# Two gather rings of four slots, a denser selection and coefficients in two halves in a PEER decoder kernel

## What is computed

```
q  = (h @ wq), split by head and in two halves
s1, s2 = scores of the halves against 128 keys each
v1, i1 = top_k(s1, 16);  v2, i2 = top_k(s2, 16)
sc, ci = top_k(v1[:, None] + v2[None, :], 16)      # of 256 candidates
eidx = i1[ci // 16] * 128 + i2[ci % 16]
gate = softmax(sc)
z    = gelu(sum_d h[d] * u_tab[eidx, d])
out  = sum_k gate[k] * z[k] * v_tab[eidx[k], :]
```

## Time and profile before

| | us |
|---|---|
| three runs, median | 2764.75 |
| lowest, highest | 2763.35, 2766.94 |
| the profiled execution | 2765.24 |
| its span | 2763.5 |
| busy: PE, DVE, POOL, ACT | 1892.6, 1378.6, 1262.6, 994.6 |

### The profile page before, as it was taken

The page is one execution under the profiler, slowest core; times in us unless marked ns, Lnnn a source line. Parts: engine busy times, 40 slices in busy tenths (PEclk is TensorE's granted clock), DMA queues, the critical chain, the costliest instruction groups (busy, mean ns, idle before and its releaser), DMA issues.

```text
span 2763.5 us, 31979 instructions
## 1 busy us (share of the span) xinstructions
PE 1892.6 (68%) x10179; PEld 1554.4 (56%) x10179; DVE 1378.6 (50%) x3350; ACT 994.6 (36%) x1254; POOL 1262.6 (46%) x1216
## 2 busy tenths in 40 slices
PE   6998855555555555699589897799556554555556
PEld 3676744444444444576389896567445443445445
DVE  1033665656555555223752534726556565656552
ACT  2102344444444443513211111213444443444445
POOL 2000677777777767300000000005777676777774
PEclk8999956666565656799689897899666665656567
DMA  9743899999999999734100002327999998999996
GB/s 360 285 153 123 307 354 352 362 335 377 342 344 340 357 354 369 290 120 166 40 1 1 1 1 73 103 80 241 362 342 373 355 367 316 364 344 377 340 357 252
DMA packets 242654, 717.42 MB, mean 260 GB/s; under 512 B 39672, under 2 KB 45056, under 8 KB 242556
## 3 DMA queue, kind: packets, MB, share of 16 engines
q0 software_dynamic: 165888, 604.05, 58.8%
q1 hardware_dynamic: 62212, 105.00, 10.8%
q10 hardware_dynamic: 14456, 7.06, 1.0%
HBM read 712.38 MB, written 3.65 MB: 259 GB/s over the span
## 4 chain that ended last, share of the span: by engine, by line
PE 37%; DMA 23%; issue 15%; POOL 12%; DVE 7%; ACT 4%; POOLq 1%; SPq 0%; DVEq 0%; ACTq 0%
PE ps L557 14%; DMA ARENA<-in_peer_u,CURU 14%; POOL ARENA L1856 12%; DMA ARENA<-in_peer_v,CURV 8%; PE ps L646 7%; PE ps L774 5%; ACT ARENA L1105 3%; DMA W<-in_w_ada 1%; PE ps L756 1%; PE ps L534 1%; PE ps L520 1%; PE ps L510 1%; DMA W<-in_conv_w_in 1%; PE ps L619 1%; DVE ARENA L1594 1%
## 5 line engine op out<-in xcount | busy, mean ns | idle before, releaser
L646 PE MATMUL ps<-ident,ARENA 128*128 128x128 f32 x4608 | 932.2, 378 | 720.2 <-ACT ARENA L1105 719.6
L646 PEld LDWEIGHTS ps<-ident,ARENA 128*128 128x128 f32 x4608 | 793.3, 199 | 859.1 <-ACT ARENA L1105 828.6
L1856 POOL DMA_INDIRECT ARENA<-in_peer_u,CURU x576 | 595.3, 1034 | 1274.4 <-DVE ARENA L1415 1079.7
L1440 DVE SCALAR_TENSOR_TENSOR ARENA<-ARENA 128x1024 f32<-128x1024 f32 x576 | 703.9, 1225 | 665.0 <-DMA ARENA<-in_peer_u,CURU 643.7
L1105 ACT ACTIVATE ARENA<-ARENA,CF 128x1024 f32<-128x1024 f32 x576 | 647.7, 1144 | 789.1 <-DMA ARENA<-in_peer_v,CURV 562.5
L1856 POOL DMA_INDIRECT ARENA<-in_peer_v,CURV x576 | 651.3, 1131 | 191.1 <-issue 164.6
L557 PE MATMUL ps<-H,W 128*128 128x288 f32 x1024 | 256.2, 414 | 4.5 <-DVEq L1785 2.8
L557 PEld LDWEIGHTS ps<-H,W 128*128 128x128 f32 x1024 | 198.6, 195 | 60.2 <-DVEq L1785 3.0
L967 ACT ACTIVATE W<-ps 128x512 f32<-128x512 f32 (+2 forms) x97 | 55.8, 578 | 233.9 <-PE ps L774 173.6
L774 PE MATMUL ps<-W 128*128 128x128 f32 (+1 forms) x1088 | 129.7, 284 | 0.1
L774 PEld LDWEIGHTS ps<-W 128*128 128x128 f32 (+1 forms) x1088 | 127.5, 199 | 2.3 <-issue 0.9
(11 more groups left out here) (281 smaller groups left out, 1616.1 us busy)
## 6 DMA issues: line engine op xcount, KB each, us to landing
W<-in_w_ada SPq DMA_DIRECT2D x24, 2048.0 KB, 15.6
W<-in_peer_wq SPq DMA_DIRECT2D x8, 2048.0 KB, 8.3
W<-in_conv_w_in SPq DMA_DIRECT2D x6, 2048.0 KB, 18.2
ARENA<-in_peer_u,CURU POOLq DMA_INDIRECT x576, 6.1
ARENA<-in_peer_v,CURV POOLq DMA_INDIRECT x576, 6.1
W<-in_conv_w_out SPq DMA_DIRECT2D x2, 2048.0 KB, 7.9
W<-in_rwkv_wr SPq DMA_DIRECT2D x2, 2048.0 KB, 25.2
W<-in_rwkv_wk SPq DMA_DIRECT2D x2, 2048.0 KB, 10.2
```

Source lines behind the costliest of these rows:

```text
L646: m = pe.matmul(ps[:, acc + c // 4, c % 4 * P:(c % 4 + 1) * P], RVV[:, k % RING, c * P:(c + 1) * P], ident[:], start=(first and k == 0 and ...
L1440: v.scalar_tensor_tensor(RU[:, k % RING, :], RU[:, k % RING, :], 1.0, h, ALU.mult, ALU.mult, accum_out=ZB[:, e, k:k + 1]).then_inc(s_z, 1)
L1856: pool.indirect_dma_start(ring[:, k % RING, :], None, tab, bass.IndirectOffsetOnAxis(ap=idx[:, k:k + 1], axis=0)).then_inc(landed[k % RING ...
```

## The change

`RING` becomes 4 for both rings. `SPAN` = 8 keeps the memory of before, so that no other buffer moves. The waits for landed tiles count four rounds of the ring in a unit. The choice gets two parts behind each of tiles 1 to 7 and behind tile 15, in place of one behind each of tiles 2 to 15. Gelu and coefficients come in halves of eight tiles: `gelu(u + 1, half 0)` ahead of V tile 10 of unit u, `coef(u + 1, half 0)` behind dot 14, the second halves at the start of the next unit (`coef` ahead of dot 3). ACT's exp comes ahead of V tile 13 in place of 14. ACT waits for the coefficients ahead of tiles 0 and 8.

```diff
-RING = 8
+RING = 4
+SPAN = 8
...
+                def gelu(u, e, half):
+                    h = slice(8 * half, 8 * half + 8)
+                    act.wait_ge(s_z, u * 16 + (8 * half + 8))
+                    act.activation(GL[:, e, h], ZB[:, e, h], ACT.Gelu).then_inc(s_gelu, 1)
+
+                gelu(u0, 0, 0)
+
                 def unit(u, lu, e, last):
-                    if not last:
+                    if last == 0:
 
                         act.wait_ge(s_sel, u * NSEL + NSEL)
                         act.sem_inc(s_actgo, 1)
                         act.activation(SCUR[:, e].rearrange("p a k -> p (a k)"), at(SCALL, lu + 2), ACT.Copy).then_inc(s_scur, 1)
-                    act.wait_ge(s_z, u * 16 + 16)
-                    act.activation(GL[:, e, :], ZB[:, e, :], ACT.Gelu).then_inc(s_gelu, 1)
-                    act.wait_ge(s_coef, u + 1)
+                    gelu(u, e, 1)
                     for k in range(TOPK):
-                        if k == 14 and not last:
+                        if k == 10 and last < 2:
+                            gelu(u + 1, 1 - e, 0)
+                        if k == 13 and last == 0:
                             gate_exp(u + 2, e)
-                        act.wait_ge(v_land[k % RING], u * 32 + 16 * (k // RING + 1))
+                        if k % 8 == 0:
+                            act.wait_ge(s_coef, u * 2 + (k // 8 + 1))
+                        act.wait_ge(v_land[k % RING], u * (16 * TOPK // RING) + 16 * (k // RING + 1))
...
                         for k in range(TOPK):
-                            if k == 2:
-                                coef(u, e)
+                            if k == 3:
+                                coef(u, e, 1)
                             if k == 8:
 
                                 v.wait_ge(s_sel, u * NSEL + 2 * NSEL)
                                 v.wait_ge(v_free, u * 16 + RING)
                                 v_indices(1 - e)
                             z_of(u + 1, k, 1 - e, at(HTOK, (lu + 1) // 8))
-                            if k >= 2:
+                            if k == 14:
+                                coef(u + 1, 1 - e, 0)
+                            if 1 <= k < 8 or k == 15:
+                                next(chosen, None)
                                 next(chosen, None)
                     else:
-                        coef(u, e)
+                        coef(u, e, 1)
                     for _ in chosen:
                         pass
-                def coef(u, e):
+
+                def coef(u, e, half):
+                    h = slice(8 * half, 8 * half + 8)
                     v.wait_ge(s_sel, u * NSEL + NSEL)
-                    v.wait_ge(s_gelu, u + 1)
-                    v.tensor_tensor(CF[:, e, :], GL[:, e, :], GATE[:, e], ALU.mult).then_inc(s_coef, 1)
+                    v.wait_ge(s_gelu, u * 2 + (half + 1))
+                    v.tensor_tensor(CF[:, e, h], GL[:, e, h], GATE[:, e, h], ALU.mult).then_inc(s_coef, 1)
+
+                coef(u0, 0, 0)
```

More of the change, by code:

```diff
@@ L144, in build @@
         W = sb("W", [WRING, DC, 512])
-        N_RV, N_ROWS, N_SEL = 2 * RING * D, 3 * D, 2880
+        N_RV, N_ROWS, N_SEL = 2 * SPAN * D, 3 * D, 2880
         ARENA = sb("ARENA", [N_RV + 2 * N_ROWS + N_SEL])
@@ L160, in build @@
         COUT = sb("COUT", [DC, 18])
-        rings = RV.rearrange("p (r s d) -> p r s d", r=2, s=RING)
+        rings = RV.rearrange("p (r s d) -> p r s d", r=2, s=SPAN)
         RU, RVV = rings[:, 0], rings[:, 1]
@@ L185, in build @@
         CROW = carve(N_RV + N_ROWS, [D])
-        KR = [carve(off, [2, HEADS, P]) for off in (RING * D + 2560, RING * D + 512)]
-        Q = carve(RING * D, [16, TOK])
-        KT = carve(RING * D + 16 * TOK, [2, HEADS, NKEYS])
+        KR = [carve(off, [2, HEADS, P]) for off in (SPAN * D + 2560, SPAN * D + 512)]
+        Q = carve(SPAN * D, [16, TOK])
+        KT = carve(SPAN * D + 16 * TOK, [2, HEADS, NKEYS])
         QP = carve(N_RV + N_ROWS, [16, P])
@@ L1108, in experts @@
                     for e in range(2):
-                        unit(i * 2 + (u0 + e), i * 2 + e, e, False)
+                        unit(i * 2 + (u0 + e), i * 2 + e, e, 0)
                 for e in range(2):
-                    unit(u0 + UNITS - 2 + e, UNITS - 2 + e, e, True)
+                    unit(u0 + UNITS - 2 + e, UNITS - 2 + e, e, 1 + e)
             def rwkv():
@@ L1437, in z_of @@
                 def z_of(u, k, e, h):
-                    v.wait_ge(u_land[k % RING], u * 32 + 16 * (k // RING + 1))
+                    v.wait_ge(u_land[k % RING], u * (16 * TOPK // RING) + 16 * (k // RING + 1))
                     v.scalar_tensor_tensor(RU[:, k % RING, :], RU[:, k % RING, :], 1.0, h, ALU.mult, ALU.mult,
```

## The result

The changed kernel takes 3145.4 us (median of 4 runs, 3141.7 to 3150.3) against 2764.1 us (2756.6 to 2766.9) for the kernel before: 1.140 times, 95% interval 1.137 to 1.143, or 381 us more. The forecast was 200 us more. The sign and the place are right; 180 us are missing, and the time lies 100 us outside the range.

The account below looks back on a forecast made before the run. The expert stages' gathers, copy engines 95% busy, were taken to bound the kernel. 31 x 1.41 + 9.6 gave 53.3 us a unit; with starts and tails 200 us more, 2765.24 + 200 = 2965 us, range 2895 to 3045.

Parts of the forecast that it names:

- The stand: Behind tile 7, DVE waits for ACT's exp and POOL stands at U12: 9.6 us between landings, 8.2 lost a unit.
- At 1.41 us a gather: Copy time of each 512 KB gather in the units, bounds 1.35 to 1.475; 31 of them plus 9.6 make 53.3 us.
- the first mark: First V index mark of layer 0: 363.9 against 338.97, 24.9 us late.
- the unit without a choice: Unit 16: dot 8 and U12 5.8 us, 22 gathers 31.0, dot 7 1.4; mark 16 at 1201.6.
- the prediction's own sum: Whole run: layer 0 93 us longer, 200 us together with layer 1, so 2965 us; chance 0.70.
- The tail: End of a layer, last dot to final reduction: V tiles alone turn in four slots, 4 us more than 24.7.
- Four slots bind nowhere in mid-unit: V slot held 9.6 us of an 11.3 us round, U slot 8.9: no cost counted in mid-unit.
- The rival of 3090 us: The four slots bind as well, V slots late in mid-unit: 125 us on top of 2965; chance 0.10.
- The halves: Gelu and coefficients in halves: ACT's 6.8 us wait goes, worth nothing by itself, but keeps four slots turning.
- The hole at the U indices: POOL's 3.3 us wait a unit goes with the denser selection: 45.1 us a unit, 2.1 to 3.1 us less.
- the rival "faster": Choice's last part falls on tile 15, so the exp wait costs nothing: 78 us gained, 2712 us; chance 0.05.
- The rival "copies run faster with fewer in flight": With four slots, copies run at 1.35 us a gather, worth 60 us: 2905 us; chance 0.10.

Follow-up runs that it names:

- the fastest kernel: Changed kernel with eight slots, the choice's last part behind tile 15 instead of 7, and h's rows copied to PSUM: 2562.8 us, 0.930 of the kernel before.

## Why the prediction was right in kind and 180 us short

**The stand: right.** The call behind tile 7 waits for the exp, DVE stands there in every unit with a choice, POOL stands at U12 (11.4 us, where I had about 9), and V12 to U12 is one chain without a copy under way. The last part behind tile 15 takes 369 us away. The term that was too small in the chain is POOL's wake-up: dot 8 is over at 489.48 and U12 is issued at 490.29, 0.8 us where I had 0.1 (from the exp to the gate sum it is 0.3 for 0.1); 10.5 us against 9.6, some 28 us over 32 units. The rows that would have told it stood in the trace of before, after the wait for L1415: DVE's L1415 ended at 739.85, POOL's gather began at 740.74.

```profile
739.68 0.17 DVE L1415 TENSOR_TENSOR ARENA<-ARENA 128x16 f32<-128x16 f32 x1
...
740.74 0.93 POOL L1856 DMA_INDIRECT ARENA<-in_peer_u,CURU  x1 [2.76 <-DVE ARENA L1415]
```

**"At 1.41 us a gather": this is the term that failed.** The period was worked out as 31 x 1.41 + 9.6, with 1.41 as what the copies can do. Measured, the 31 others take (57.8 - 10.5)/31 = 1.53 us, 3.6 us a unit and some 115 us in 32 units more than forecast. In layer 0, 93 us were missing: 8 at the first mark, 68 in the 15 units (3.6 of each 4.5 by this term, 0.9 by the chain), 9 in the unit without a choice and 8 in the tail. The copies' share of 0.95 misled: it went with 354 GB/s, and 1.01 goes with 402, so a share near one did not mean that no more could be moved. The pace came from POOL, whose issue of 0.94 + 0.30 us grows when it meets a dot.

Counted over the timeline of layer 0 from 324 us on: before, the 107 issues with at most 0.05 us of a dot beside them took 0.937 us on average and the 445 others 1.115; after, 177 took 0.940 and 381 took 1.218, as dots released in a row behind the gate fall on issues more fully (0.60 us of overlap against 0.53). With h in PSUM (the fastest kernel) 401 issues overlap a dot and take 0.944.

The earlier trace rows had it in plain sight: POOL's mean of 1034 ns beside the single issue of 0.94 in the earlier trace rows have POOL busy for 525.78 of 723 us; with 0.3 us behind each of some 480 issues and the 50.2 us of the earlier trace rows that is the whole window. I read past it.

The rivals come apart by this. Dots as a load on DVE's time: no, the 1.22 us dots of the PSUM kernels take 7 to 33 us more than the short ones (the 33 in the changed kernel, where dot 8 is in the chain), of 80 to 162 gained. Copies as the limit: no, 1.30 us a gather once POOL is free. TensorE, whose granted clock is 0.53 in the units in place of 0.61: no, POOL waits 0.3 us a unit for transposes. Two SBUF inputs against POOL's issue: yes.

With the hold-ups taken out, the prediction's own sum is met, in part by luck. In the changed kernel with h in PSUM the first mark is at 365.5 (forecast 363.9), the period 52.8 us (53.3; the wake-up of 0.8 and a gather at 1.365 nearly cancel), mark 16 at 1202.6 (1201.6; the unit without a choice takes 45.6 in place of 38.2 and makes up for the 15 shorter ones), and the whole 2983 us (2965). The hold-ups are 3145 - 2983 = 162 us of the 180.

**The tail: too small.** "4 us more" behind the last dot was 12.5: in the changed kernel the last dot starts at 1307.93 and the last reduction at 1345.09, 37.2 us against 24.7 in the earlier trace rows and 28.7 forecast (36.9 with h in PSUM). V tiles alone turn in four slots in rounds of 11.4 us (scaling of three in a row at 1320.90 and at 1332.30), where I had 6.9; what the 4.5 us more consist of was not taken apart. That is 8.4 us in layer 0, some 17 in all, and with the 162 it makes up the 180.

```profile
1307.93 1.23 DVE L1450 SCALAR_TENSOR_TENSOR ARENA<-ARENA 128x1024 f32<-128x1024 f32 x1 [1.74 <-DMA ARENA<-in_peer_u,CURU]
...
1320.90 3.66 ACT L1115 ACTIVATE ARENA<-ARENA,CF 128x1024 f32<-128x1024 f32 x3 [2.03 <-DMA ARENA<-in_peer_v,CURV]
...
1332.30 3.65 ACT L1115 ACTIVATE ARENA<-ARENA,CF 128x1024 f32<-128x1024 f32 x3 [2.15 <-DMA ARENA<-in_peer_v,CURV]
...
1345.09 1.23 DVE L1524 TENSOR_REDUCE ARENA<-ps 128x256 f32<-128x1024 f32 x1 [35.41 <-PE ps L647]
```

**Four slots bind nowhere in mid-unit: right for this kernel**, by 0.3 us a unit of waits for transposes and by the pair with the gate at tile 15, 0.3 us a unit apart in layer 0 and 1.0 in layer 1. The rival of 3090 us came nearer to the time by chance, not by its mechanism. Four slots alone cost 6.7%, but at the head of the unit, where the rival didn't look.

**The halves: nothing alone, right. The hole at the U indices: 2.1 to 3.1 us a unit was forecast, and 2.3 was there.** The dense selection alone brings 2.2% of the 2752.8 us of before beside it, 53 us, where the rival "faster" had 78 for the hole; its first mark comes 7 us later than before (346.0 against 339.0). But the forecast of 45.1 us a unit was met (45.5 and 45.2) for another reason than it gave: POOL's issues are longer there, 1.12 us, and with 0.30 behind each they fill 45.4 us with no wait left.

**The rival "copies run faster with fewer in flight": wrong.** The copies can go at 1.30 us, but it is a free POOL that lets them, with eight slots. With four and a free POOL it was 1.365.

**Still open:** why the full stretch of before stops at 389 GB/s where the PSUM kernel holds 402. No run takes that apart. Nor was it shown which of POOL's reads the dot holds up; that it is the indices is argued from the instruction, not measured. And no run tells why an issue needs 0.81 us more once the dot is over.

## What to carry to other kernels

A wait placed in an in-order engine's loop costs what the ring behind it cannot cover: the same wait cost 48 us with eight slots and 369 with four, so price a wait and the ring's depth together. A copy queue that is 95% busy need not be the limit: add up the issuing engine's busy time and the short rests between its issues, leave out its real waits, and see how much of the period that fills; then compare its mean duration with its shortest. If an issue on POOL is stretched beside DVE work, move one of DVE's two inputs to PSUM, which cost a copy of h once a tile of tokens here and brought 3 to 5%.

## What the runs showed of the hardware

- An indirect gather's issue on POOL lasts 0.94 us and its successor starts 0.30 us later, 1.24 us for 128 rows of 4 KB. Beside a DVE product of two SBUF inputs it lasts 1.12 to 1.22 us on average. One that begins while the product runs ends 0.81 us after the product does (226 of 231 issues before, 194 of 197 after, within 0.01 us), so it lasts up to 1.99 us when the two begin together; one that a product meets only after its first 0.2 us lasts 0.94 (168 issues before, 0.95 at most). With one of the inputs in PSUM and the same 1.22 us of DVE time it lasts 0.94 (401 issues of the fastest kernel). The Trainium skill, "SBUF — State Buffer", section "Who interferes with whom", says that a DVE instruction with two SBUF inputs contends with a GpSimd instruction that reads SBUF, since its second input comes through the read interface that the two share; these rows agree, as far as a gather's issue is an instruction that reads SBUF (its indices lie there).
- One core's gathers of 512 KB ran at 402 GB/s over 680 us, 1.30 us each (h in PSUM, eight slots).
- POOL took 0.8 us from the end of the dot it waited for to its next issue, after a stand of 11 us, and 0.9 us after one of 2.8 us in the kernel before (739.85 to 740.74).
